# Earlier rounding of the second weight unit of two feed-forwards, and inverse roots taken in two halves

## The reference, cut to what matters

```python
# block 1, behind its mixer
x = layer_norm(DEEPNORM_ALPHA * x + (1.0 + g1) * y, ln1_g, ln1_b)
h = x * (1.0 + sc2) + sh2
ff = square(relu(h @ w_ff_in)) @ w_ff_out          # 1024 -> 4096 -> 1024
x = layer_norm(DEEPNORM_ALPHA * x + (1.0 + g2) * ff, ln2_g, ln2_b)
# block 2
p = rms_norm_2(x, norm1_g) @ w_in
q = rms_norm_2(p[..., 0:512] by heads of 64, q_norm_g)
k = rms_norm_2(p[..., 512:1024] by heads of 64, k_norm_g)
...
x = x + mix @ w_out
x = x + square(relu(rms_norm_2(x, norm2_g) @ w_mlp1)) @ w_mlp2
```

## Time and profile before

| | |
|---|---|
| three runs | 1543.73, 1537.9, 1545.56 us |
| profiled execution, its own time | 1541.47 us |
| its span in the trace | 1539.7 us |
| TensorE matmul busy | 1452.9 us, 94% |
| VectorE, ScalarE, GpSimd busy | 686.7, 514.8, 652.7 us |
| mean granted clock of TensorE | 0.969 of full speed |
| waits of TensorE for a weight remainder | 17.4 us, 6 times |

### The profile page before, as it was taken

One profiled execution on the slowest core, in us unless ns is written; L12 is line 12 of the kernel. 1 busy time (PEld: TensorE's weight loads), 2 busy tenths in 40 slices (PEclk: granted clock), 3 DMA queues, 4 the chain that ended last, 5 costly groups with the idle time before them and its releaser, 6 DMA issues.

```text
span 1539.7 us, 17538 instructions
## 1 busy us (share of the span) xinstructions
PE 1452.9 (94%) x6751; PEld 1191.7 (77%) x6751; DVE 686.7 (45%) x1011; ACT 514.8 (33%) x739; POOL 652.7 (42%) x518
## 2 busy tenths in 40 slices
PE   3998999999998988999999997989999999999999
PEld 2786788787877877888888886876888788888887
DVE  6574766488851477213141347226632313222131
ACT  1544343344422515223141323423434323223230
POOL 1442244433222475454545454471223544545352
PEclk9997999999997998999999998999999999999999
DMA  9251434444521332323232323220102232232322
GB/s 332 84 139 55 109 111 163 137 158 132 163 69 55 108 114 82 110 82 109 84 107 87 104 88 104 82 82 28 55 32 79 84 108 92 98 100 91 109 82 82
DMA packets 119991, 157.38 MB, mean 102 GB/s; under 512 B 5196, under 2 KB 81248, under 8 KB 119936
## 3 DMA queue, kind: packets, MB, share of 16 engines
q1 hardware_dynamic: 117744, 151.15, 30.6%
q0 software_dynamic: 1648, 5.39, 1.1%
q10 hardware_dynamic: 544, 0.10, 0.0%
HBM read 154.45 MB, written 2.17 MB: 102 GB/s over the span
## 4 chain that ended last, share of the span: by engine, by line
PE 83%; DVE 5%; POOL 4%; ACT 3%; issue 2%; DMA 1%; SPq 1%; POOLq 0%; DVEq 0%; ACTq 0%
PE bank L1413 24%; PE bank L1414 24%; PE bank L1415 24%; PE bank L1557 3%; POOL w_lo L483 3%; PE bank L1748 3%; PE bank L1547 1%; DMA raw<-in_w_in_dram 1%; PE bank L1887 1%; POOL head_rs L467 1%; PE bank L1668 1%; ACT w_hi L609 1%; SPq L368 1%; ACT arena L661 0%; DVE early L1116 0%
## 5 line engine op out<-in xcount | busy, mean ns | idle before, releaser
L483 POOL TENSOR_TENSOR w_lo<-raw,w_hi 128x512 fp32r<-128x512 f32 x432 | 584.7, 1386 | 684.9 <-ACT w_hi L609 684.9
L1413 PE MATMUL bank<-w_hi,a_hi 128*128 128x512 f32 x928 | 367.6, 396 | 3.8 <-DVE a_lo L923 2.9
L1414 PE MATMUL bank<-w_lo,a_hi 128*128 128x512 f32 x928 | 365.1, 393 | 0.0
L1415 PE MATMUL bank<-w_hi,a_lo 128*128 128x512 f32 x928 | 364.6, 393 | 0.0
L609 ACT ACTIVATE w_hi<-raw 128x2048 fp32r<-128x2048 f32 x108 | 206.5, 1913 | 395.3 <-PE bank L1415 360.5
L1413 PE MATMUL bank<-a_hi,w_hi 128*128 128x512 f32 x800 | 319.3, 399 | 16.4 <-POOL w_lo L483 14.7
L1414 PE MATMUL bank<-a_lo,w_hi 128*128 128x512 f32 x800 | 315.4, 394 | 0.0
L1415 PE MATMUL bank<-a_hi,w_lo 128*128 128x512 f32 x800 | 315.2, 394 | 0.0
L1413 PEld LDWEIGHTS bank<-w_hi,a_hi 128*128 128x128 f32 x928 | 177.0, 191 | 45.9 <-issue 5.7
L1415 PEld LDWEIGHTS bank<-w_hi,a_lo 128*128 128x128 f32 x928 | 176.6, 190 | 37.5
L1414 PEld LDWEIGHTS bank<-w_lo,a_hi 128*128 128x128 f32 x928 | 176.8, 191 | 36.3
(11 more groups left out here) (216 smaller groups left out, 1155.1 us busy)
## 6 DMA issues: line engine op xcount, KB each, us to landing
raw<-in_w_in_dram SPq DMA_DIRECT2D x32, 1024.0 KB, 5.3
raw<-in_w_mlp_dram SPq DMA_DIRECT2D x32, 1024.0 KB, 5.2
arena<-in_w_ada_dram SPq DMA_DIRECT2D x18, 1024.0 KB, 5.2
raw<-in_w_ff_in_dram SPq DMA_DIRECT2D x16, 1024.0 KB, 5.2
raw<-in_w_ff_out_dram SPq DMA_DIRECT2D x16, 1024.0 KB, 5.1
raw<-in_w_out_dram SPq DMA_DIRECT2D x12, 1024.0 KB, 5.1
arena<-in_w_ada_dram SPq DMA_DIRECT2D x3, 2048.0 KB, 18.0
early<-acs_d SPq DMA_DIRECT2D x4, 1024.0 KB, 9.7
```

The lines of the kernel that those rows point to most:

```text
L483: last = pool.tensor_tensor(w_lo[:, u0 % 2, cols], raw[:, u0 % 2, cols], w_hi[:, u0 % 2, cols].bitcast(F32), ALU.subtract)
L1413: pe.matmul(out_, hi_a, hi_b, start=start, stop=False)
L1414: pe.matmul(out_, hi_a, lo_b, start=False, stop=False)
L1415: return pe.matmul(out_, lo_a, hi_b, start=False, stop=stop)
```

## The change

Four things are done. The rounding of the second unit of both feed-forwards moves ahead on ScalarE: for the first to ahead of `turned_affine`, for the second to between the fourth and the fifth turned tile. Its remainder moves ahead on GpSimd: for the first to ahead of the clearing of `yacc` and the two DMAs, for the second to ahead of the roots. In the loops over quarters each pass now ends with the second unit of the next quarter instead of beginning with its own, and the last quarter stands outside the loop. The 64 inverse roots become two instructions of 32, one for queries ahead of `lo(U_QKV2 + 4)` and one for keys ahead of `lo(U_CP)`, and VectorE waits for each by itself.

```diff
--- before.py
+++ after.py
@@ -466,6 +466,11 @@
                 link(pool.tensor_scalar(st2[:, o:o + n], src, scale, eps, ALU.mult, ALU.add))
                 pool.tensor_tensor(dst, st2[:, o:o + n], nhalf[:, 0:n], ALU.pow).then_inc(signal, 1)
 
+            def head_root(n):
+                pool.wait_ge(qk_sq, n + 1)
+                part = head_rs[:, 32 * n:32 * n + 32]
+                inv_root(32, part, part, 1.0 / HD, EPS2, qk_rs, 32 * n)
+
             def rms_root(turn, eps):
                 pool.wait_ge(y_sq, 4 * turn + 4)
                 inv_root(4, st[:, 0:4], st[:, 4:8], 1.0 / D, eps, rs_made)
@@ -566,15 +571,18 @@
             lo(U_WO2 + 4)
             ln_root(0)
             pool.wait_ge(xhat_made, 4)
+            lo(U_FF1 + 1)
             pool.memset(yacc, 0.0).then_inc(acc0, 1)
 
-            def feed_forward(u0, times):
-                with pool.Fori(0, times) as i:
+            def feed_forward(u0, n_last):
+                with pool.Fori(0, QUARTERS - 1) as i:
                     for b in range(8):
-                        lo(u0 + b + 1, i, 8)
+                        lo(u0 + b + 2, i, 8)
+                for b in range(n_last):
+                    lo(u0 + 8 * (QUARTERS - 1) + b + 2)
 
             relative_tiles()
-            feed_forward(U_FF1, QUARTERS)
+            feed_forward(U_FF1, 7)
             load_row(1, ln2_g)
             load_row(2, ln2_b)
             ln_root(1)
@@ -583,18 +591,17 @@
             lo(U_QKV2 + 1)
             lo(U_QKV2 + 2)
             rms_root(2, EPS2)
-            for u in range(U_QKV2 + 3, U_CP):
+            lo(U_QKV2 + 3)
+            head_root(0)
+            for u in range(U_QKV2 + 4, U_CP):
                 lo(u)
-            pool.wait_ge(qk_sq, 2)
-            inv_root(64, head_rs[:], head_rs[:], 1.0 / HD, EPS2, qk_rs)
-            for u in range(U_CP, U_FF2 + 1):
+            head_root(1)
+            for u in range(U_CP, U_FF2 + 2):
                 lo(u)
             rms_root(3, EPS2)
             pool.wait_ge(rs_made, 4)
             pool.tensor_tensor(st[:, 12:16], st[:, 4:8], st[:, 4:8], ALU.mult).then_inc(r2_made, 1)
-            feed_forward(U_FF2, QUARTERS - 1)
-            for b in range(7):
-                lo(U_FF2 + 8 * (QUARTERS - 1) + b + 1)
+            feed_forward(U_FF2, 6)
 
         @block.scalar
         def _(act):
@@ -660,21 +667,22 @@
                     act.wait_ge(pt_t, 3 * h + m + 1)
                     act.activation(dst[:, 512 * m:512 * m + n * P], bank[b][:, 0:n * P], ACT.Copy).then_inc(pt_made, 1)
 
-            def feed_forward(u0, m0, n0, i, last):
+            def feed_forward(u0, m0, n0, i, units):
 
                 for b in range(2):
                     for j in range(4):
-                        if j % 2 == 0:
-                            hi(u0 + 2 * b + j // 2 + 1, i, 8)
+                        if j == 2:
+                            hi(u0 + 2 * b + 2, i, 8)
+                        elif b and j == 0:
+                            hi(u0 + 3, i, 8)
                         k = 4 * b + j
                         act.wait_ge(ticks, at(i, 16, 2 * (u0 + 2 * b) + j + 1))
                         act.wait_ge(tile_made, at(i, 8, m0 + k - 1))
                         act.activation(rl[:, k % 2], bank[4 * b + j][:], ACT.Relu).then_inc(evac[b], 1)
                         act.wait_ge(evac[b], at(i, 8, 4 * n0[b] + j + 1))
                         act.activation(a_hi[1][:, k], rl[:, k % 2], ACT.Square).then_inc(a_hi_made, 1)
-                for b in range(4, 8):
-                    if not (last and b >= 7):
-                        hi(u0 + b + 1, i, 8)
+                for b in range(5, units):
+                    hi(u0 + b, i, 8)
 
             def small_vectors():
                 act.wait_ge(cleared, 2)
@@ -847,9 +855,11 @@
             hi(U_WO2 + 2)
             hi(U_WO2 + 3)
             hi(U_WO2 + 4)
+            hi(U_FF1 + 1)
             turned_affine(R_X1, T_X1, 0, lambda k: mod[:, 48 + k:49 + k], lambda k: mod[:, 56 + k:57 + k])
-            with act.Fori(0, QUARTERS) as i:
-                feed_forward(U_FF1, M_HID1, N_FF1, i, False)
+            with act.Fori(0, QUARTERS - 1) as i:
+                feed_forward(U_FF1, M_HID1, N_FF1, i, 10)
+            feed_forward(U_FF1, M_HID1, N_FF1, QUARTERS - 1, 9)
             hi(U_QKV2 + 1)
             turned_affine(R_N2, T_N2, 0, lambda k: mod[:, 64 + k:65 + k], lambda k: mod[:, 72 + k:73 + k])
             junk = view(10240, D)
@@ -895,11 +905,13 @@
             for b in range(1, 4):
                 hi(U_WO3 + b + 1)
             for k in range(KT):
+                if k == 4:
+                    hi(U_FF2 + 1)
                 turned_hi(R_N3, 0, k, N3_BANKS[k], v1[:, V_N2 + k:V_N2 + k + 1])
             squares(3, x1, junk, evac[0], lambda t: 4 * (N_WO3[0] + 1))
             with act.Fori(0, QUARTERS - 1) as i:
-                feed_forward(U_FF2, M_HID2, N_FF2, i, False)
-            feed_forward(U_FF2, M_HID2, N_FF2, QUARTERS - 1, True)
+                feed_forward(U_FF2, M_HID2, N_FF2, i, 10)
+            feed_forward(U_FF2, M_HID2, N_FF2, QUARTERS - 1, 8)
 
         @block.vector
         def _(dve):
@@ -1248,8 +1260,8 @@
                     dve.reduce_sum(head_rs[:, 32 * n:32 * n + 32], sq2.rearrange("p t (h d) -> p (t h) d", d=HD), AX)\
                         .then_inc(qk_sq, 1)
                     dve.wait_ge(qk_sq, n + 1)
-                dve.wait_ge(qk_rs, 1)
                 for n in range(2):
+                    dve.wait_ge(qk_rs, n + 1)
                     q = qkv2[:, n].rearrange("p t (h d) -> p (t h) d", d=HD)
                     dve.tensor_tensor(q, q, head_rs[:, 32 * n:32 * n + 32].unsqueeze(2).broadcast_to([P, 32, HD]), ALU.mult)\
                         .then_inc(qk_made, 1)
```

## The result

The changed kernel took 1520.68 us (median of five runs, 1519.61 to 1527.66) against 1543.73 us (median of five, 1537.9 to 1550.62). The ratio is 0.9864, with a 95% interval of 0.9837 to 0.9890: 1.4% faster, 1521 us having been forecast. The profiled execution was the slowest of the five, 1527.66 us with a span of 1525.9, so absolute positions in its trace are not those of the median. One execution of the loops alone, further down, took 1883.28 us at a granted clock of 0.73 and is left out of its ratio.

What follows compares the result with a forecast made beforehand. TensorE was taken to bound the kernel, with gaps at three places. Waits of 4.7 + 5.6 + 4.2 = 14.5 us plus 6.9 of clock make 21.4 us, giving 1521 us, 1.4% faster, range 1515 to 1531.

Steps and rivals of the forecast that it cites:

- The bound: Whole kernel: TensorE, matmuls busy 94% of the span, sets the time; only filling its gaps or restoring its clock pays.
- The sum: All three places: 14.5 us of waits and 6.9 of clock, 21.4 us, giving 1521 us, 1.4% faster.
- First feed-forward: Unit 1, head of first feed-forward: remainder ready at about 579.3, 4.73 us of wait gone; unit 2 late by at most 1.2.
- signs of being wrong: Powers over 7 us each, unit 2 of first feed-forward or last values' unit waiting, or TensorE idling at a quarter boundary.
- Queries and keys: First unit of the further columns: two powers of 32 at 5.6 us let it start at 1020.6, 5.6 us earlier.
- Second feed-forward: Unit 1 of second feed-forward: remainder ready at 1187.2, before unit 0 ends at 1192.3; gain 4.2 us.
- Loops: Loops over quarters: queue order stays, only the boundary of a pass moves; costed at nothing.
- The clock: Behind the three gaps: half-clock matmuls lose 2.6, 2.1 and 2.2 us; all 6.9 counted as won, bound none.
- Only the waits go: Rival, three gaps: slow matmuls come elsewhere, so only 14.5 us of waits go, 1527 us; chance 0.12.
- A shared port gives part back: Rival, last values' unit and unit 2 of first feed-forward: late remainders give back 4.9 us, 1525 us; chance 0.11.
- Nothing changes: Rival, unit 1: the remainder is not the last wait and another holds it, 1541 us; chance 0.04.
- slower: Rival, six quarter boundaries: second unit late, 6.8 us each, 41 in all, 1561 us; chance 0.03.

Runs made afterwards that it cites:

- the loops alone: Kernel before with only the loops over quarters rewritten; second unit's rounding and remainder at old places, roots one instruction of 64; ratio 1.0009 to before.
- the queries first: Changed kernel with VectorE multiplying the queries by their roots ahead of squaring the keys; 0.9822 of before, 0.9861 when run again.
- loops and roots alone: Kernel before with rewritten loops and the roots of queries and keys taken apart, both feed-forwards rounding their second unit late; ratio 0.9951 to before.

## Why the prediction was right

**The bound.** Right. TensorE set the end, and all that was won at the three places stayed to the end: "others" moves by at most 3.4 us between any two profiles, and from `U_FF2 + 3` to the last rounding it is 303.5 us in all of them.

**The sum.** 21.4 us were forecast; the stages lose 21.8 against before and 21.6 against the loops alone. That the median, 1520.68, lies 0.3 us from the 1521 is luck: two more sets of the same kernel had medians of 1527.08 and 1525.03. The three terms were 7.3, 7.7 (5.6 and 2.1) and 6.4 us, and 8.0, 7.2 and 6.6 came, so their errors partly cancel.

**First feed-forward.** 4.7 of wait and 2.6 of clock, 7.3, were forecast; 7.1 to 8.0 came. Unit 2 was named as the next late thing, with 0 to 1.2 us; it was 0.3. Taken by the letter, a wait of unit 2 was one of the signs of being wrong; this one lies within the bound that was given for it. The remainder beside `split_affine` took 4.98 us with L935 at 0.75, as the row of the second norm had said. One thing in this step was superfluous: GpSimd's move was taken as part of it, and the kernel without it has the same 132.2 us.

**Queries and keys.** The power of 32 columns, in no row of before, was put at 5.6 us from the slope of two others and takes 5.43. The gain in start was 5.2 us (a wait of 6.08 became 0.88), not 5.6; TensorE starts 0.46 us behind the last read of the values. I let the keys' roots begin at 1006.1, the end of `lo(U_QKV2 + 5)` without disturbance, and one paragraph on let the same remainder end at 1007.9 beside the multiplication. The sum should have used the second, which gives 1021.2 for the start and 5.0 us of gain. Timelines of GpSimd and VectorE of the changed kernel (they answer to the earlier trace rows):

```profile
982.31 5.43 POOL L467 TENSOR_TENSOR head_rs<-st,nhalf 128x32 f32<-128x32 f32 x1
987.71 5.02 POOL L488 TENSOR_TENSOR w_lo<-raw,w_hi 128x512 fp32r<-128x512 f32 x4
998.28 7.55 POOL L488 TENSOR_TENSOR w_lo<-raw,w_hi 128x512 fp32r<-128x512 f32 x4 [5.55 <-ACT w_hi L616]
...
1001.15 3.44 POOL L488 TENSOR_TENSOR w_lo<-raw,w_hi 128x512 fp32r<-128x512 f32 x1
...
1011.62 7.06 POOL L488 TENSOR_TENSOR w_lo<-raw,w_hi 128x512 fp32r<-128x512 f32 x4
...
1001.15 2.29 DVE L1266 TENSOR_TENSOR arena<-arena,head_rs 128x2048 f32<-128x2048 f32 x1
...
1011.69 3.37 DVE L1266 TENSOR_TENSOR arena<-arena,head_rs 128x2048 f32<-128x2048 f32 x1 [8.26 <-POOL head_rs L467]
```

The fourth row is one of the four instructions of the third. The last remainder of the values took 7.55 us in place of 5.41 and ended at 1005.83, while TensorE was free for its unit at 1005.81 and took it at 1005.88. The price of one multiplication was 2.1 us where 1.8 had been taken (the quotient given there, (9.2 - 5.4) / 2, is 1.9). The Trainium skill, "SBUF — State Buffer", section "Who interferes with whom", says that the port pair which the two engines share is an exclusive lock, and that the order of issue decides who blocks. The trace agrees: the first multiplication, at 1001.15, kept its 2.29 us, and the GpSimd instruction that started with it took 3.44 us in place of 1.29. The second started 0.07 us behind a GpSimd instruction and took 3.37 us itself, 1.08 more than the first. `lo(U_CP)` beside one multiplication was put at 7.3 and took 7.06.

**Second feed-forward.** 4.2 and 2.2 forecast, 6.6 measured. Here both moves were needed for the whole gain, as the prediction had them.

**Loops.** Costed at nothing; 1.0009, with an interval on both sides of 1.

**The clock.** The bound that nothing of the 6.9 us comes back is ruled out: the stages won 21.6 to 21.8 us where the waits alone are 13.5 against before (14.1 against the loops alone). That leaves 7.5 to 8.3 us for the clock.

**The rivals.** "Only the waits go" fell. "A shared port gives part back" happened in kind, 2.1 us for one remainder, but cost TensorE only some 0.4 us through the keys' roots: with the queries first the stage is 0.4 us shorter. "Nothing changes" fell with the ratio, whose interval ends at 0.9890, and "slower" with the loops alone and with 314.0 of 314.0 us busy from 610 on.

## What to carry to other kernels

When a weight passes through several queues, write down for each queue where its instruction stands and what it waits for; the unit is ready behind the last of them, and only that one need move (first feed-forward), unless another stands right behind it (second). Price a gap of TensorE with the matmuls at half clock behind it, here 2 to 4 us on top of gaps of 4 to 6. When a wait is taken away, look at what the released instruction now runs beside: its own duration may stay while its neighbour's grows, and that neighbour's later end belongs in the sum.

## What was not expected of the hardware

Most of the spread between runs of one program goes with the granted clock of TensorE. In the nine sets of six to twelve runs a run's time and its mean granted clock are correlated at -0.87 to -0.98. The same head took 516.9 to 531.2 us in fourteen profiles; in its window 200:560 the clock was 0.98 in the two shortest, with 1772 matmuls each, and 0.92 in the longest, with 1701. Why the clock falls in one execution and not in the next is not shown. Medians of five or six runs of the changed kernel lay 6.4 us apart. Stages marked by a common instruction tell more: in the projection 61.4 us came three times with the change and 61.0 three times with the queries first. They have their own spread too, 0.6 to 0.9 us in the first feed-forward for the same code.

The half clock also does not follow a gap at once each time. In the kernel with loops and roots alone TensorE waited 3.78 us ahead of unit 1 of the second feed-forward and started again at full rate; the clock fell some 1.5 us later, with the matmuls running (the window 1185.6:1187 has a clock of 1.00, 1187:1189 of 0.52). Timeline of TensorE and, in the second fence, two windows of that kernel:

```profile
1185.65 0.50 PE L1425 MATMUL bank<-a_hi,w_hi 128*128 128x512 f32 x1 [3.78 <-POOL w_lo L488]
```

```profile
1185.60:1189.00 3.40, 3.35 (x11) 2.64 (x12) 2.12 (x2) 0.00 (x0) 3.40 (x3) 0.72 0.59 164
1189.00:1193.00 4.00, 4.00 (x16) 3.24 (x15) 0.00 (x0) 0.00 (x0) 2.46 (x2) 0.81 0.51 135
```

That stage took 43.1 us where the same code took 44.0 and 44.2 in other profiles. In the changed kernel gaps of 0.29 and 0.88 us left the clock at 1.00.
